# Four chains of a recurrence's chunk stages, started two rounds apart instead of in lockstep

## The reference

```
def step(S, inp):
    w_t, k_t, v_t, a_t, b_t = inp[:5]
    sa = jnp.einsum('bhij,bhj->bhi', S, a_t)
    S = S * w_t[:, :, None, :] + sa[..., None] * b_t[:, :, None, :] + v_t[..., None] * k_t[:, :, None, :]
    y = jnp.einsum('bhij,bhj->bhi', S, inp[5]) if emit else None
    return S, y
S, ys = lax.scan(step, state0, xs, reverse=reverse)
```

## Time and profile before

| | |
|---|---|
| median of 3 runs | 2348.21 us (2344.32 to 2349.25) |
| profiled execution | 2346.54 us, span 2344.7 us |
| busy share of the span: PE, PEld, DVE, ACT, POOL | 75%, 51%, 35%, 28%, 9% |
| instructions: PE, PEld, DVE, ACT, POOL | 16973, 16973, 1177, 1054, 206 |
| granted TensorE clock, mean | 0.86 of full |
| transfers | 588.7 MB, 251 GB/s over the span |
| chunk stages | 866 to 912, 933 to 977, 1121 to 1169.5 and 1194 to 1241 us |

### The profile page before, as it was taken

The page is one execution under the profiler, slowest core; times in us unless marked ns, Lnnn a source line. Parts: engine busy times, 40 slices in busy tenths (PEclk is TensorE's granted clock), DMA queues, the critical chain, the costliest instruction groups (busy, mean ns, idle before and its releaser), DMA issues. The chain is left out here.

```text
span 2344.7 us, 38529 instructions
## 1 busy us (share of the span) xinstructions
PE 1769.6 (75%) x16973; PEld 1196.1 (51%) x16973; DVE 824.0 (35%) x1177; ACT 648.6 (28%) x1054; POOL 218.9 (9%) x206
## 2 busy tenths in 40 slices
PE   6999988988999876698788977565665655565565
PEld 6997986867778765597677852111111111111111
DVE  4654445765555565477464542000000000000001
ACT  4434445554333354334452330000000000000001
POOL 0100014420121031000330000000000000000000
PEclk9999998999999877899796988878778788788867
DMA  6654642246986410061002459999999999999997
GB/s 207 197 180 144 197 154 73 88 138 225 317 274 218 158 51 3 5 202 59 4 3 85 154 212 392 429 428 428 427 428 428 428 428 428 428 428 428 428 428 312
DMA packets 178994, 588.74 MB, mean 251 GB/s; under 512 B 8179, under 2 KB 141374, under 8 KB 154126
## 3 DMA queue, kind: packets, MB, share of 16 engines
q1 hardware_dynamic: 177458, 585.38, 64.8%
q10 hardware_dynamic: 1372, 0.92, 0.2%
HBM read 584.99 MB, written 1.28 MB: 250 GB/s over the span
## 5 line engine op out<-in xcount | busy, mean ns | idle before, releaser
L3386 PE MATMUL ps<-ex_ring,ex_xe 128*32 128x512 f32 x1440 | 224.8, 757 | 158.6 <-DMA ex_ring<-in_exp_w 158.6
L3467 DVE TENSOR_TENSOR ex_hid<-ps,ex_silu 128x512 f32<-128x512 f32 x16 | 11.1, 692 | 865.6 <-PE ps L3386 865.6
L3386 PEld LDWEIGHTS ps<-ex_ring,ex_xe 128*32 128x32 f32 x1440 | 44.1, 125 | 336.2 <-DMA ex_ring<-in_exp_w 244.8
L209 PE MATMUL ps<-xt_hi,ffn_whi 128*128 128x256 f32 x704 | 204.1, 290 | 7.3 <-DVE xt_lo L372 7.3
L210 PE MATMUL ps<-xt_lo,ffn_whi 128*128 128x256 f32 x704 | 199.7, 284 | 0.0
L211 PE MATMUL ps<-xt_hi,ffn_wlo 128*128 128x256 f32 x704 | 199.5, 283 | 0.0
L181 DVE TENSOR_TENSOR ffn_wlo<-ring,ffn_whi 128x2048 fp32r<-128x2048 f32 x66 | 154.3, 2338 | 112.7 <-ACT ffn_whi L174 112.2
L3408 PE MATMUL ps<-ex_ring,ex_ht 128*32 128x512 f32 x688 | 118.2, 821 | 77.8 <-DMA ex_ring<-in_exp_w 73.0
L174 ACT CAST ffn_whi<-ring 128x2048 fp32r<-128x2048 f32 x66 | 125.2, 1901 | 110.2 <-PE ps L211 95.9
L209 PEld LDWEIGHTS ps<-xt_hi,ffn_whi 128*128 128x128 f32 x704 | 136.5, 194 | 17.5 <-issue 15.6
L210 PEld LDWEIGHTS ps<-xt_lo,ffn_whi 128*128 128x128 f32 x704 | 136.1, 193 | 1.5 <-issue 1.5
(11 more groups left out here) (772 smaller groups left out, 3952.0 us busy)
## 6 DMA issues: line engine op xcount, KB each, us to landing
ex_ring<-in_exp_w SPq DMA_DIRECT2D x133, 2048.0 KB, 46.3
ring<-in_exp_w SPq DMA_DIRECT2D x39, 2048.0 KB, 45.7
ring<-in_w_in SPq DMA_DIRECT2D x55, 1024.0 KB, 5.2
ex_late<-in_exp_w SPq DMA_DIRECT2D x19, 2048.0 KB, 46.3
ring<-in_ffn_w_gate SPq DMA_DIRECT2D x22, 1024.0 KB, 6.2
ring<-in_ffn_w_up SPq DMA_DIRECT2D x22, 1024.0 KB, 5.4
ring<-in_ffn_w_down SPq DMA_DIRECT2D x22, 1024.0 KB, 5.0
ffn_mod_tile<-in_mod_w SPq DMA_DIRECT2D x12, 1024.0 KB, 7.2
```

The costliest lines, as they stand in the source:

```text
L209: nc.tensor.matmul(out, lhs[0], rhs[0], start=start, stop=False, skip_group_check=shared)
L3386: mm = mm_(ps[32 * q:32 * q + 32, 4 + u, :], xe[:, k], w[:, 512 * q:512 * q + 512], start=k == 0, stop=k == KC - 1)
L3467: v.tensor_tensor(hid[:], ps[:, 5, :], silu[:], ALU.mult).then_inc(S["hid"], 1)
```

## The change

order() no longer runs in lockstep. With BEHIND = 2 it goes through 13 + 2 x 3 = 19 steps, and in step s it yields for each chain q the round s - 2q, where that is a round. So q0 does rounds 0 and 1 alone, q1 joins in step 2, q2 in step 4, q3 in step 6; q0 is done after step 12, q3 after step 18. All four chains are under way only in steps 6 to 12. GpSimd's expand and join are interleaved to match. No instruction is added or removed, no wait either.

```
+BEHIND = 2
...
         def order():
-            for r in range(CHUNK_ROUNDS):
-                for q in range(len(its)):
-                    yield q, r
+            for step in range(CHUNK_ROUNDS + BEHIND * (NQ - 1)):
+                for q in range(NQ):
+                    r = step - BEHIND * q
+                    if 0 <= r < CHUNK_ROUNDS:
+                        yield q, r
...
+            expand(0)
             for q in range(NQ):
-                expand(q)
-            if not ctx_only:
-                for q in range(NQ):
+                if q + 1 < NQ:
+                    expand(q + 1)
+                if not ctx_only:
                     join(q)
```

## The result

The changed kernel takes 2373.16 us (median of 4 runs, 2369.8 to 2378.26) against 2346.74 us (median of 4 runs of before): the ratio is 1.0108, 95% interval 1.0085 to 1.013. It is slower, by 26 us where 12 were forecast, and 2 us outside the range. The profiled execution has a span of 2369.0 us, 24.3 us over before.

A forecast was written before the change was run, and what follows sets the result against it. The experts' weight stream, bound by bytes, ends the kernel, and chunk stages set its start. Per stage 9.0 more waits - 5.6 stops - 0.6 stage end = +2.8, rounded to 3; 4 x 3 = 12 us gives 2360 us, range 2350 to 2371.

The forecast's parts named there:

- The experts' stream is the end, and a stage's delay passes to it in full: Last 960 us, experts' weights: bound by bytes; a chunk stage 1 us longer moves the end by 1 us.
- TensorE is held to 256 instructions per 3.6 us: TensorE in chunk stages: stopped until its next instruction block has come, 0.85 to 1.4 us where nothing else is awaited.
- The stops shrink by 5.6 us a stage, from 10.3 to 4.7: TensorE's stops for instruction blocks in rl0c: partly hidden under the new waits, so 5.6 us less.
- The rival in which they don't shrink: Rival 3: waits hide no stops, +8.4 us a stage, 34 over four, 2382 us; chance not stated separately.
- the one in which they pay for all: Rival 2: waits hide under block stops, up to -8 us, say 2343; faster 0.07, within 0.2% 0.10.
- The end of the stage gives back 0.6 us: Stage end: VectorE has one chain's last eviction behind TensorE's last product, not four; 1.3 us instead of 1.9.
- GpSimd costs nothing: GpSimd's expand, joins, tm and last g2 in a stage: all hidden under other rounds, no cost.
- Sum: 10.6 + 2.1 = 12.7 us, against 3.7: 9.0 more: TensorE's waits in rl0c: 10.6 us at first rounds plus 2.1 at the far end, against 3.7 in lockstep.
- the first two entries, 2.7 and 1.6: Chain q0 in rl0c, nothing in between: waits 2.7 us from round 0 to 1, 1.6 from round 1 to 2.
- time from the end of that until the next round may start, if nobody else is in the way: List per round of a chain in rl0c: 2.7 us after round 0, 1.6, 1.5, then 0.6 to 1.1.
- handovers: Between engines in a chain's round: 0.3 us allowed in the list after rounds 1 and 2, 0.2 for one.
- The range's upper end (2371): Whole kernel: top of the range said to hold 8 in 10, which runs from 2350 to 2371 us.

The follow-up runs named there:

- the doubled products: Lockstep order, with the products of rounds 5 to 8 issued twice in every chunk stage: ratio 1.0237, 55.6 us over before.
- The filler runs: Lockstep plus one small product behind each chain's products in rounds 5 to 8: ratio 1.0027 with another tile shape, 1.0019 with the same.

## Why the prediction was wrong

Point by point, by its own steps:

- The experts' stream is the end, and a stage's delay passes to it in full: right (25.4 us at the stream, 24.3 in the span).
- TensorE is held to 256 instructions per 3.6 us: right, shown by the doubled products (3.55 us per block).
- The stops shrink by 5.6 us a stage, from 10.3 to 4.7: right in size (11.6 to 6.0 in the mean of the split above, 5.6 less). That it is 5.6 again is luck: the figure was worked out for rl0c, where they shrank by 4.7. The rival in which they don't shrink falls, and so does the one in which they pay for all.
- The end of the stage gives back 0.6 us: 0.5.
- GpSimd costs nothing: right (its order alone, 0.9993).
- **The failing step is the sum of what a stage loses at round starts**, "Sum: 10.6 + 2.1 = 12.7 us, against 3.7: 9.0 more". Idle at round starts went from 6.6 to 19.3 us a stage, 12.7 more. The list of waits was right in its sum: the first two entries, 2.7 and 1.6, were 2.8 and 1.9, others were off by some tenths in either direction, and all waits of a stage sum to about 12.7 us, the forecast figure (before they were 5.2, not 3.7, so they grew by 7.5 and not 9.0). What the list puts at nothing is the idle time at a change of tile shape: 25 more changes a stage, and with them 5.8 us a stage behind the arrival of the operands, against 0.7. The two make up the growth, 7.5 + 5.1. In "time from the end of that until the next round may start, if nobody else is in the way", I took every round to follow the one before at once if its operands were there. In lockstep that is nearly true, with three changes a stage, so the trace of before hardly shows the price. The timeline of before did have its 0.2 us at those places, and I took them for handovers.
- What follows: 12.7 - 5.6 - 0.5 - 0.5 (issue) is 6.1 us a stage and 24.3 us for four, where I had 3 and 12. The range's upper end (2371) was set by half of a rival with another mechanism, and the result is just outside.

What stays open is how the net loss of 24 us divides between waits and changes of shape. Both are idle time at round starts, and the stops paid for 22 of the 51 us that were added there; no run has the staggered order without the changes. The filler runs show the price of a change but hide it in stops.

## What to carry to other kernels

Before staggering chains on an engine that works in order, list for each chain what stands between one of its rounds and the next, in the new order: if lockstep already covers the longest eviction with the other chains' work, the stagger only opens holes. If it must be staggered, put the newest chain's long first round ahead of the others in a step. Count how often the new order changes TensorE's tile shape, and look whether idle time is paid by the stops between blocks of instructions or adds to them; a phase of many small products is limited by the number of its instructions first.

## What the runs showed of the hardware that was not expected

- A change between 128x32, 32x32, 32x64 and 64x32 weights leaves TensorE's weight loads idle for 0.13 to 0.54 us even with all operands there; 0.20 or 0.25 us into a 128x32 filler and 0.15 us out of it, against 0.00 to 0.08 into one of the same shape. It goes with the granted clock: of the 12 changes from rounds 1 to 4 to a round 0 in the changed kernel, the 6 with 0.54 us stand where TensorE was granted 1.2 GHz and the 6 with 0.29 us where it was granted 2.4 GHz. The lower level stands in the first steps of each stage (866.0 to 883.0 us in rc0c).
- 256 TensorE instructions come no faster than every 3.45 to 3.6 us here, 13.5 to 14 ns each. In the chunk stages before, TensorE stood still for 46 of 175 us because of it, more than for all evictions. The Trainium skill's page "Runtime: NRT & Kernel Launch" (instruction fetch mechanics) calls the cost of crossing into the next block mostly hidden; the doubled products say otherwise.
